# Fifteen taps of one 31-tap convolution chunk as diagonal fp32 products on the matmul engine

## The chip, the cores and the metric

One core of a Trainium2 chip. The metric is the device time of one execution in microseconds. TensorE is called PE, VectorE DVE, ScalarE ACT, GpSimd POOL, SyncE SP.

## The reference, cut to what matters

Two transformer blocks over 512 tokens of width 1024. The second begins with a mixer of two halves: a causal depthwise convolution of 31 taps over 512 channels, followed by a layer norm over the channels and SiLU, and an mLSTM of four heads. Both halves are joined and multiplied by `w_out`; a mixture of 32 experts follows.

```python
u = conv_a * jax.nn.sigmoid(conv_gate)
u = causal_depthwise_conv(u, conv_w, conv_b)      # width 31, one filter per channel
u = jax.nn.silu(layernorm(u, conv_ln_g, conv_ln_b))
...
y = jnp.concatenate([u, hm], axis=-1)             # hm: the four mLSTM heads
return jnp.einsum("bse,ed->bsd", y, w_out)
```

All values are fp32.

## The kernel before

Activations lie transposed: 128 features on the partitions, 512 tokens along a row, one such array being a chunk. The convolution has four chunks (0 to 3), the mLSTM one chunk per head (0 to 3). A product with weights is made from two fp32r parts of either operand, as three matmuls (hi*hi, hi*lo, lo*hi, `terms`, L96). Products of plain fp32 operands take two passes, which the profile shows as two matmuls.

Weight tiles come through a ring of four slots (`ring_load`, L847). `ring_split` (L854) makes the two parts of a tile: ACT copies it to fp32r (L861), POOL subtracts (L864). It is called two tiles ahead, when PE has finished a tile. The mixer has 24 tiles (0 to 23, L1328), made by `feature_tile` (L1256) and `value_tiles` in banks 6, 7 and 2 to 5. `take` (L1275) empties a bank; for the `a` tile of chunk n it writes the gated input `u_pad`, padded by 30 zeros in front, and opens the generator `conv_taps(n)` (L1034): one ACT instruction for tap 0 and the bias, then 30 DVE instructions `dst += w_j * u_pad[j : j + 512]` (L1043), each waiting for the one before.

Eight tiles of the output product follow (24 to 31, `out2_tile`, L1346), as (half i of the output's columns, pair of input chunks). Order: (0,2), (0,3), (1,2), (1,3), (0,0), (0,1), (1,0), (1,1). Pairs 2 and 3 are the heads, pairs 0 and 1 the convolution. Each tile is made in four quarters of 128 tokens, six matmuls each; with pair 2 the residual is added through eight small matmuls with the identity per quarter (L1379). Tile 24's last quarter uses a bank that head 3's sums occupy and waits for `taken[3]`; tile 26's last quarter uses bank 7, where the convolution's layer norm makes its sums, and waits for `stats_read`. Tile 25 needs head 3's split, tile 28 the splits of convolution chunks 0 and 1, tile 29 those of 2 and 3.

The order of instructions in every engine's queue is set while the program is built. `clk` holds an estimated clock for PE, ACT and DVE, `est` adds a cost to one, and background work is written as generators that yield the time at which they want to go on. `tick(spent)` (L1227) is called between groups of matmuls: it adds the time to PE's clock, resumes each background generator that is due, and then emits taps as long as DVE's clock is less than 0.8 beyond PE's. Two open convolution chunks give their taps in turn. `until` (L1251) ticks by 0.3 until a thing it needs has been emitted. An engine executes its queue in order, and waits for others through semaphores.

The generators in this stretch are:
- `weigh(h)` (L1053) for head h: scores (L1063), DVE scaling (L1072), products with the values and with ones (L1078, L1081)
- `finish(h)` (L1130): absolute value on ACT (L1134), gate and maximum on DVE (L1136, L1138, `taken`), the sum over features on PE (L1144), centring on DVE (L1148), squares on ACT (L1151, L1153), their sum on PE (L1159), DVE (L1163), square root on ACT (L1166), reciprocal and multiply on DVE (L1169, L1170), split (L313 on ACT, L315 on DVE)
- `conv_norm()` (L1189), which starts when all four chunks are in `convolved`: mean product (8 passes, the first L460 group in the rows), centring on DVE (L1201), squares on ACT (L1202), squares product, statistics (L1209, `stats_read`), square root, reciprocal, and per chunk multiply (L1217), SiLU (L1219) and split.

When tile 27 is done SP loads the first four expert weights of 2 MB (L1410, in the trace L921), when tile 31 is done three more (L1435); the expert stage follows.

Of the kernel before, what the change touches and what calls it, by code (L numbers as in the profile page):

```python
# [21 lines left out]
T, D = 512, 1024  # L22
# [6 lines left out]
CONV_W, QKC_W = 31, 4  # L29
# [15 lines left out]
ACT, ALU, AX = mybir.ActivationFunctionType, mybir.AluOpType, mybir.AxisListType  # L45
# [83 lines left out]
def build(nc, x_d, cols_d, rows_d, wdense_d, wff_d, wif_d, wr_d, strips_d, experts_d, out_d):  # L129
    sem = nc.alloc_semaphore  # L130
    PE = Queue("pe", nc.tensor, sem("pe_steps"))
    AC = Queue("ac", nc.scalar, sem("act_steps"))
    DV = Queue("dv", nc.vector, sem("dve_steps"))
    PO = Queue("po", nc.gpsimd, sem("pool_steps"))
    SP = Queue("sp", nc.sync, None)
    pe, ac, dv, po, sp = nc.tensor, nc.scalar, nc.vector, nc.gpsimd, nc.sync
# [14 lines left out]
    def sb(name, words, dt=F32, parts=128):  # L151
        return nc.alloc_sbuf_tensor(name, [parts, words], dt)

    def sb2(name, words):

        t = sb(name, words)
        return t, nc.alloc_sbuf_tensor_at(name + "_parts", [128, words], F32R, offset=nc.sbuf_base - words * 4)
# [3 lines left out]
    ident, ones, tri, tri_strict = sb("ident", 128), sb("ones", 128), sb("tri", 128), sb("tri_strict", 128)  # L161
# [8 lines left out]
    att, att_r = sb2("attention_buffers", 8 * T)  # L170
    hi_raw, weights_hi = sb2("weights_hi", 2 * SLOT)
    sumsq, rinv = sb("sum_of_squares", T), sb("token_scale", T)
    banks = [nc.alloc_psum_tensor(f"bank{i}", [128, 512], F32) for i in range(8)]
# [4 lines left out]
    def col(name, k=0):  # L178
        return cols[:, COLS[name] + k:COLS[name] + k + 1]

    def chunk(t, k, n=T, w=T, off=0):

        return t[:, bass.ds(k * w + off, n)]
# [300 lines left out]
    at = {}  # L484
    n = 0
# [349 lines left out]
    clk, due = {"pe": 0.0, "ac": 0.0, "dv": 0.0}, [0.0]  # L835

    def est(q, cost, after=0.0):

        clk[q] = max(clk[q], after or due[0] or clk["pe"]) + cost
        return clk[q]  # L840
# [4 lines left out]
    ring_freed, hi_made, lo_made = {}, {}, {}  # L845
# [33 lines left out]
    m = pe.matmul(banks[0][:, :], ones[:, :], sumsq[:, :], start=True, stop=True)  # L879
# [46 lines left out]
    PU, PQ = T + CONV_W - 1, T + QKC_W - 1  # L926
    at_ = 0

    def part(n):
        nonlocal at_  # L930
        at_ += n
        assert at_ <= BIG - 8 * T
        return big[:, at_ - n:at_]
    u_pad, qk_pad = part(4 * PU), part(4 * PQ)
# [4 lines left out]
    ym = part(8 * T)  # L939
# [15 lines left out]
    dense_read, gated, padded, tapped, convolved, opened = [None] * 8, {}, {}, {}, {}, {}  # L955
    scored, summed_up, taken, var_read, split, split_u, silus = {}, {}, {}, {}, {}, {}, {}
    v2_ready, rows_ready, sig_read, stats_read = [], [], [selectors], {}
    floored = {}
    next_taps, x_ready = [], []
    dense_done, rows_at, taps_at, tick_at = [], [], {}, []  # L960


# [71 lines left out]
    def conv_taps(c):  # L1034

        AC.wait(gated[c])
        last = AC.step(ac.activation(chunk(ym, c), u_pad[:, c * PU:c * PU + T], ACT.Identity,  # L1037
                                     scale=col("conv_w", c * CONV_W), bias=col("conv_b", c)))
        began = est("ac", 0.65)
        for j in range(1, CONV_W):  # L1040
            src, w, dst = u_pad[:, c * PU + j:c * PU + j + T], col("conv_w", c * CONV_W + j), chunk(ym, c)
            DV.wait(last, gated[c] if j == 1 else None)
            last = DV.step(dv.scalar_tensor_tensor(dst, src, w, dst, ALU.mult, ALU.add))  # L1043
            clk["dv"] = max(clk["dv"], began) + 0.85
            yield
        convolved[c] = last


    weights = [W(3), W(4)[:, 0:384], W(5)[:, 0:256], W(4)[:, 384:512]]
# [175 lines left out]
    background, short_taps, long_taps, started, ticks = [], [], [], [0], []  # L1225
# [30 lines left out]
    def feature_tile(i, kind, n):  # L1256

        w = ring_tile(i)
        bank = 6 + i % 2
        PE.wait(dense_read[bank])  # L1260
        for k in range(KD):
            ts = terms(w[:, k * 128:(k + 1) * 128], chunk(nrm_parts, k))
            for j, (x, y_) in enumerate(ts):
                if not ring_freed:
                    PE.wait(ready[k])
                m = pe.matmul(banks[bank][:, :], x, y_, start=k + j == 0, stop=k == KD - 1 and j == 2, skip_group_check=True)  # L1266
            if k == KD - 1:
                if kind in "qk" and n >= 2:
                    until(tapped, n - 2)
                take(kind, n, ring_done(i, m), bank)  # L1270
                ring_split(i + 2)
            if k % 2:
                tick(1.38)

    def take(kind, n, r, bank):  # L1275

        if kind != "a":
            AC.wait(r)
        if kind == "g":
            AC.wait(sig_read[0])  # L1280
            dense_read[bank] = opened["g", n] = AC.step(ac.activation(sumsq[:, :], banks[bank][:, :], ACT.Sigmoid,
                                                                      bias=col("b_conv", 4 + n)))
            est("ac", 2.0)
        elif kind == "a":
            DV.wait(r, opened["g", n])
            gated[n] = sig_read[0] = dense_read[bank] = DV.step(dv.scalar_tensor_tensor(
                u_pad[:, n * PU + CONV_W - 1:(n + 1) * PU], banks[bank][:, :], col("b_conv", n), sumsq[:, :],
                ALU.add, ALU.mult))
            est("dv", 0.8)
            long_taps.append(conv_taps(n))  # L1290
        elif kind == "o":
            dense_read[bank] = opened["o", n] = AC.step(ac.activation(o_gate[n], banks[bank][:, :], ACT.Sigmoid,
                                                                      bias=col("b_o", n)))
            est("ac", 2.0)
        else:
            r_ = kind == "k"
            p0 = (2 * (n % 2) + r_) * PQ
            AC.wait(tapped.get(n - 2))
            dense_read[bank] = padded[kind, n] = AC.step(ac.activation(
                qk_pad[:, p0 + QKC_W - 1:p0 + PQ], banks[bank][:, :], ACT.Identity, bias=col("b_qk", n + 4 * r_)))  # L1300
            est("ac", 0.7)
            if kind == "k":
                next_taps.append(n)
# [100 lines left out]
    for n, (i, pair) in enumerate(tiles):  # L1404
# [16 lines left out]
        if n == 7:  # L1421
            PE.wait(*out_copied[0])
            for k in range(4):
                bank = banks[sums_at[0][k]]
                for t in range(NT):
                    m = pe.transpose(bank[:, t * 128:(t + 1) * 128], x_tok[:, t * D + k * 128:t * D + (k + 1) * 128], ident[:, :])
# [14 lines left out]
    def half_logits(t, i):  # L1441

        return product(halves_of_logits[i][:, t, 0:36],
                       [(h_feat[:, k * T + t * 128:k * T + (t + 1) * 128], wr[:, k * 36:(k + 1) * 36])
                        for k in range(4 * i, 4 * i + 4)])
# [17 lines left out]
    for t in range(NT):  # L1463
        m = half_logits(t, 0)
# [22 lines left out]
    for t in range(NT):  # L1487
        PO.wait(AC.step(ac.activation(h_tok[:, t * D:(t + 1) * D], x_tok[:, t * D:(t + 1) * D], ACT.Identity,
                                      scale=st[:, t:t + 1])))
# [76 lines left out]
    m = pe.matmul(banks[0][:, 0:NT * 32], tri_strict[:, :], both, start=True, stop=False, skip_group_check=True)  # L1566
    for d in range(1, NT):
        m = pe.matmul(banks[0][:, d * 32:NT * 32], ones[:, :], both[:, 0:(NT - d) * 32], start=False, stop=d == NT - 1,
                      skip_group_check=True)
# [351 lines left out]
    for t in range(NT):  # L1921
        for j in range(2):
            c = j * NT + t
# [145 lines left out]
```

How the kernel before makes its waits and increments, by code:

```python
    def run(self, ins):  # L114
        s = self.step(ins)
        self.eng.wait_ge(self.sem, s.value(self.loop))
        return s
# [1 line left out]
    def wait(self, *steps):  # L120
        for s in steps:
            if s is not None:
                self.eng.wait_ge(s.queue.sem, s.value(self.loop))
# [5 lines left out]
def build(nc, x_d, cols_d, rows_d, wdense_d, wff_d, wif_d, wr_d, strips_d, experts_d, out_d):  # L129
# [77 lines left out]
    cleared = PO.run(po.memset(zeros, 0.0))  # L207
    PO.run(po.affine_select(out=ident[:, :], in_=ident[:, :], compare_op=ALU.not_equal, fill=1.0, base=0,
                            pattern=[[-1, 128]], channel_multiplier=1))
    PO.run(po.affine_select(out=tri[:, :], in_=ones[:, :], compare_op=ALU.is_ge, fill=0.0, base=0,
                            pattern=[[1, 128]], channel_multiplier=-1))
    c_ready = PO.run(po.affine_select(out=tri_strict[:, :], in_=ones[:, :], compare_op=ALU.is_gt, fill=0.0,
                                      base=0, pattern=[[1, 128]], channel_multiplier=-1))
    for q in (PE, AC, DV):
        q.wait(c_ready)
        q.eng.wait_ge(s_cols, 16)
    iota_f, tok_id, fold = sb("iota_f", 128), sm(2 * NT), sm(2 * BS)
    PO.run(po.tensor_tensor(fold, ident[:, 0:2 * BS], ident[:, 2 * BS:4 * BS], ALU.add))
    PO.run(po.iota(iota_f[:, :].bitcast(I32), [[1, 128]], base=0, channel_multiplier=0))
# [272 lines left out]
    for k in range(KD):  # L493
        if k % 2 == 0:
            ac.wait_ge(s_x[k // 2], 16)
            dv.wait_ge(s_x[k // 2], 16)
# [32 lines left out]
    dv.wait_ge(s_strip, 16)
    for hh in range(12):
```

## Time and profile before

| | |
|---|---|
| median of three runs | 2053.32 us (2043.6 to 2054.55) |
| profiled execution, its time | 2054.98 us |
| its span, first to last instruction | 2053.7 us |
| mean granted clock of PE | 0.937 |
| PE busy | 1824.7 us (89%) |
| DVE busy | 863.6 us (42%) |
| ACT busy | 432.7 us (21%) |
| POOL busy | 992.7 us (48%) |

The span is 1.3 us shorter than the profiled execution's own time. PE is busy for most of the span, but its load is not even: the mixer and output product lie between about 1190 and 1500 us, the expert stage with its weight transfers behind that. Busy shares say little about one stretch; there the chain that ended last and the timelines of the engines are to be read. Matmuls overlap each other by about 0.17 us in the rows, so the distance of their starts counts, not the sum of their times. The granted clock is 1.00 at 2.4 GHz and 0.50 at 1.2 GHz.

### The profile page before, as it was taken

Reading aid. Unit: us, or ns where it says so; the run is one execution under the profiler, and the core shown is the slowest. Engines: PE = TensorE matmul, PEld = TensorE weight load, DVE = VectorE, ACT = ScalarE, POOL = GpSimd, SP = SyncE. Lnnn points to the kernel's source line nnn. Section 1 sums busy time; section 2 is a strip of 40 time slices with the busy share of each in tenths; the row PEclk is TensorE's granted clock in tenths of the full one; section 3 lists DMA queues with packets and bytes.
Section 4 is the critical chain, followed back from the end, with each engine's and each line's share of the span. In section 5 each row is a group of like instructions: output and inputs, shape, how many; then the busy total and the mean of one; then the engine's idle time right before and its main releaser. Section 6 shows DMA issues by size and latency. Waiting matters only on the chain.

```text
span 2053.7 us, 27415 instructions
## 1 busy us (share of the span) xinstructions
PE 1824.7 (89%) x9686; PEld 1287.1 (63%) x9686; DVE 863.6 (42%) x1256; ACT 432.7 (21%) x794; POOL 992.7 (48%) x536
## 2 busy tenths in 40 slices
PE   5999999989999899999999798996877978969783
PEld 4888888877776578888888666664642423323331
DVE  5444443410254567444444489877341111111113
ACT  3111100100244432111100143551321211111112
POOL 5888887767544278888888523321211111101101
PEclk9999999999999999999999999997868988988897
DMA  3333363423221123333333222210579999999983
GB/s 126 97 97 93 105 262 98 141 79 98 66 62 52 32 85 95 97 93 101 92 109 98 72 60 64 72 52 21 212 287 412 374 408 402 410 415 398 413 358 133
DMA packets 56977, 346.00 MB, mean 168 GB/s; under 512 B 8474, under 2 KB 8858, under 8 KB 44896
## 3 DMA queue, kind: packets, MB, share of 16 engines
q1 hardware_dynamic: 44640, 315.12, 42.1%
q10 hardware_dynamic: 7968, 19.46, 2.6%
q0 software_dynamic: 4320, 10.78, 1.5%
q8 instruction: 29, 0.48, 0.1%
q14 instruction: 20, 0.16, 0.0%
HBM read 475.06 MB, written 19.66 MB: 241 GB/s over the span
## 4 chain that ended last, share of the span: by engine, by line
PE 70%; DMA 13%; DVE 11%; ACT 3%; issue 1%; POOL 1%; SPq 0%; DVEq 0%; ACTq 0%; POOLq 0%
PE bank L460 31%; DMA big<-w_up_in 13%; PE bank L431 12%; PE bank L1760 7%; PE bank L692 4%; PE bank L1266 3%; DVE big L1043 3%; PE bank L1778 2%; PE bank L479 2%; PE bank L1376 2%; PE bank L1786 1%; PE bank L610 1%; DVE state L1028 1%; PE bank L670 1%; PE bank L1678 1%
## 5 line engine op out<-in xcount | busy, mean ns | idle before, releaser
L277 POOL TENSOR_TENSOR weights_hi_parts<-ring,ones 128x1024 fp32r<-128x1024 f32 (+1 forms) x176 | 356.6, 2026 | 304.7 <-PE bank L460 139.1
L279 POOL TENSOR_TENSOR ring_parts<-ring,weights_hi_parts 128x1024 fp32r<-128x1024 f32 (+1 forms) x176 | 473.9, 2693 | 13.8
L460 PE MATMUL bank<-attention_buffers_parts,weights_hi_parts 128*128 128x512 f32 x832 | 329.4, 396 | 27.9 <-POOL ring_parts L279 17.6
L460 PE MATMUL bank<-state_parts,weights_hi_parts 128*128 128x512 f32 x832 | 326.8, 393 | 0.0
L460 PE MATMUL bank<-attention_buffers_parts,ring_parts 128*128 128x512 f32 x832 | 326.7, 393 | 0.0
L1760 PE MATMUL bank<-big,work 128*32 128x512 f32 x1440 | 231.7, 685 | 54.5 <-DMA big<-w_up_in 54.4
L431 PE MATMUL bank<-big_parts,weights_hi_parts 128*128 128x512 f32 x704 | 217.1, 389 | 1.2 <-POOL ring_parts L279 1.2
L460 PEld LDWEIGHTS bank<-attention_buffers_parts,weights_hi_parts 128*128 128x128 f32 x832 | 158.1, 190 | 64.6 <-POOL ring_parts L279 17.6
L864 POOL TENSOR_TENSOR ring_parts<-ring,weights_hi_parts 128x1024 fp32r<-128x1024 f32 x32 | 81.0, 2534 | 234.1 <-ACT weights_hi_parts L861 234.1
L1860 POOL TENSOR_TENSOR small<-small 128x1 f32<-128x1 f32 x51 | 9.7, 190 | 381.3 <-DVE small L1683 381.3
L460 PEld LDWEIGHTS bank<-state_parts,weights_hi_parts 128*128 128x128 f32 x832 | 158.3, 190 | 33.4 <-issue 0.8
L460 PEld LDWEIGHTS bank<-attention_buffers_parts,ring_parts 128*128 128x128 f32 x832 | 158.0, 190 | 33.5
L1719 DVE TENSOR_TENSOR work<-bank,cols 128x256 f32<-128x256 f32 x54 | 22.9, 425 | 306.0 <-PE bank L1678 304.9
L431 PEld LDWEIGHTS bank<-big_parts,weights_hi_parts 128*128 128x128 f32 x704 | 132.0, 188 | 29.2 <-POOL ring_parts L279 2.0
L1760 PEld LDWEIGHTS bank<-big,work 128*32 128x32 f32 x1440 | 63.6, 123 | 135.3 <-issue 129.6
L431 PE MATMUL bank<-big_parts,ring_parts 128*128 128x512 f32 x352 | 136.9, 389 | 0.0
L406 DVE TENSOR_TENSOR work<-bank,token_scale 128x512 f32<-128x512 f32 x44 | 30.4, 692 | 199.9 <-PE bank L460 199.9
L1043 DVE SCALAR_TENSOR_TENSOR big<-big,cols 128x512 f32<-128x512 f32 x120 | 106.5, 929 | 6.4 <-ACT big L1037 5.3
L315 DVE TENSOR_TENSOR big_parts<-work,big_parts 128x512 f32 (+1 forms) x44 | 82.9, 1884 | 42.3 <-ACT big_parts L313 42.3
L1792 ACT ACTIVATE weights_hi<-bank 128x512 f32<-128x512 f32 x54 | 32.3, 598 | 312.1 <-PE bank L1760 312.1
L1760 PE MATMUL bank<-attention_buffers,work 128*32 128x512 f32 x288 | 75.0, 667 | 24.0 <-DMA big<-w_up_in 23.4
L313 ACT ACTIVATE big_parts<-work 128x512 f32 (+1 forms) x44 | 27.9, 633 | 287.3 <-DVE work L408 287.3
(377 smaller groups left out, 2827.1 us busy)
## 6 DMA issues: line engine op xcount, KB each, us to landing
big<-w_up_in SPq DMA_DIRECT2D x54, 2048.0 KB
ring<-wdense_in SPq DMA_DIRECT2D x176, 512.0 KB, 3.6
state<-w_down_in SPq DMA_DIRECT2D x37, 2048.0 KB
big<-w_gate_in SPq DMA_DIRECT2D x36, 2048.0 KB
attention_buffers<-w_gate_in SPq DMA_DIRECT2D x18, 2048.0 KB
ring<-w_down_in SPq DMA_DIRECT2D x18, 2048.0 KB
ring<-wff_in SPq DMA_DIRECT2D x32, 704.0 KB, 4.1
y_rows<-big ACTq DMA_DIRECT2D x1, 8192.0 KB, 28.0
```

The source lines that it names most:

```text
L277: po.tensor_tensor(hi, raw, ones[:, 0:1].to_broadcast([128, words]), ALU.mult).then_inc(PO.sem, 1)
L279: po.tensor_tensor(lo, raw, hi.bitcast(F32), ALU.subtract) \
L315: return DV.step(dv.tensor_tensor(lo, raw, hi.bitcast(F32), ALU.subtract))
L431: m = pe.matmul(bank, x, y_, start=t + k + n == 0, stop=t == 1 and k == h - 1 and n == 2)
L460: m = pe.matmul(out, x, y_, start=j + n == 0, stop=j == len(pairs) - 1 and n == len(ts) - 1)
L479: m = pe.matmul(banks[t][:, :], x, y_, start=k + n == 0, stop=k == KD - 1 and n == len(ts) - 1)
L692: m = pe.matmul(banks[7][:, :], x, y_, start=k + t == 0, stop=k == KD - 1 and t == 2, skip_group_check=True)
L864: lo_made[n] = PO.step(po.tensor_tensor(lo, raw, hi.bitcast(F32), ALU.subtract))
L1043: last = DV.step(dv.scalar_tensor_tensor(dst, src, w, dst, ALU.mult, ALU.add))
L1266: m = pe.matmul(banks[bank][:, :], x, y_, start=k + j == 0, stop=k == KD - 1 and j == 2, skip_group_check=True)
L1376: m = pe.matmul(bank[:, :], x, y_, start=k == 4 and n == 0, stop=k == 3 and n == 2, skip_group_check=True)
L1760: m = pe.matmul(first_products[b][p:p + BS, :], xet[:, (k + odd) * BS:(k + odd + 1) * BS], sets[b][m_][:, (k + odd) * D_EXP:(k + odd + 1) ...
```

## The change

The DVE taps of convolution chunk 3 stop 15 earlier. Once the mixer's last tile is done, ACT makes 15 diagonal matrices of 128x128 in `att`, which held an operand of the mixer: the identity, each row scaled by that channel's weight of taps 16 to 30. PE multiplies each with the shifted input and sums all 15 products in bank 7; plain fp32, so two passes each. One DVE instruction adds the bank to the 16 taps that ACT and DVE made. The generator `pe_taps` emits five diagonals per tick, then one product per tick, and adds 0.88 per product to PE's estimated clock. `convolved[3]` is now set by the addition.

```diff
--- before.py
+++ after.py
@@ -956,7 +956,7 @@
     scored, summed_up, taken, var_read, split, split_u, silus = {}, {}, {}, {}, {}, {}, {}
     v2_ready, rows_ready, sig_read, stats_read = [], [], [selectors], {}
     floored = {}
-    next_taps, x_ready = [], []
+    next_taps, x_ready, own_taps, PE_TAPS = [], [], [], 15
     dense_done, rows_at, taps_at, tick_at = [], [], {}, []
 
 
@@ -1037,13 +1037,46 @@
         last = AC.step(ac.activation(chunk(ym, c), u_pad[:, c * PU:c * PU + T], ACT.Identity,
                                      scale=col("conv_w", c * CONV_W), bias=col("conv_b", c)))
         began = est("ac", 0.65)
-        for j in range(1, CONV_W):
+        for j in range(1, CONV_W - (PE_TAPS if c == 3 else 0)):
             src, w, dst = u_pad[:, c * PU + j:c * PU + j + T], col("conv_w", c * CONV_W + j), chunk(ym, c)
             DV.wait(last, gated[c] if j == 1 else None)
             last = DV.step(dv.scalar_tensor_tensor(dst, src, w, dst, ALU.mult, ALU.add))
             clk["dv"] = max(clk["dv"], began) + 0.85
             yield
-        convolved[c] = last
+        if c < 3:
+            convolved[c] = last
+        else:
+            own_taps.append(last)
+
+    def pe_taps():
+
+        while not dense_done:
+            yield 0
+        AC.wait(gated[3], ring_freed[23])
+        made = []
+        for n in range(PE_TAPS):
+            d = att[:, n * 128:(n + 1) * 128]
+            made.append(AC.step(ac.activation(d, ident[:, :], ACT.Copy, scale=col("conv_w", 3 * CONV_W + CONV_W - PE_TAPS + n))))
+            at = est("ac", 0.33)
+            if n % 5 == 4:
+                yield 0
+        PE.wait(dense_read[7])
+        for n in range(PE_TAPS):
+            j = 3 * PU + CONV_W - PE_TAPS + n
+            PE.wait(made[n])
+            m = pe.matmul(banks[7][:, :], att[:, n * 128:(n + 1) * 128], u_pad[:, j:j + T], start=n == 0, stop=n == PE_TAPS - 1,
+                          skip_group_check=True)
+            clk["pe"] += 0.88
+            if n < PE_TAPS - 1:
+                yield 0
+        m = PE.step(m)
+        at = clk["pe"]
+        while not own_taps:
+            yield 0
+        yield at
+        DV.wait(m, own_taps[0])
+        convolved[3] = DV.step(dv.tensor_tensor(chunk(ym, 3), chunk(ym, 3), banks[7][:, :], ALU.add))
+        est("dv", 0.8)
 
 
     weights = [W(3), W(4)[:, 0:384], W(5)[:, 0:256], W(4)[:, 384:512]]
@@ -1288,6 +1321,8 @@
                 ALU.add, ALU.mult))
             est("dv", 0.8)
             long_taps.append(conv_taps(n))
+            if n == 3:
+                background.append([pe_taps(), 0.0])
         elif kind == "o":
             dense_read[bank] = opened["o", n] = AC.step(ac.activation(o_gate[n], banks[bank][:, :], ACT.Sigmoid,
                                                                       bias=col("b_o", n)))
```

## Rows read from the trace of the kernel before

**Rows 1.** The page, section 4: the chain that ended last, share by engine.

```profile
PE 70%; DMA 13%; DVE 11%; ACT 3%; issue 1%; POOL 1%; SPq 0%; DVEq 0%; ACTq 0%; POOLq 0%
```

**Rows 2.** The chain from 1376 to 1500: start us, us, what.

```profile
1388.87 3.27 DVE work L1169
...
1428.16 0.76 DVE big L1043
...
1429.17 3.69 PE bank L460 x8
...
1444.66 5.49 PE bank L1376 x24
...
1450.25 1.06 ACT weights_hi_parts L861
...
1457.29 19.31 PE bank L1376 x72
```

**Rows 3.** Timeline of PE, 1376 to 1444: start, us, instructions, [idle before <-releaser].

```profile
1379.29 0.67 PE L1063 MATMUL bank<-state 128*128 128x256 f32 x2 [1.96 <-DVE work L1072]
...
1383.25 1.02 PE L1159 MATMUL bank<-state,ones 128*128 128x512 f32 x2
...
1395.78 0.79 PE L1376 MATMUL bank<-weights_hi_parts,big_parts 128*128 128x512 f32 x1 [3.85 <-DVE work L1138]
...
1403.41 1.13 PE L1159 MATMUL bank<-state,ones 128*128 128x512 f32 x2 [1.45 <-ACT state L1151]
1413.95 0.79 PE L1376 MATMUL bank<-weights_hi_parts,big_parts 128*128 128x512 f32 x1 [9.41 <-DVE big_parts L315]
...
1429.17 3.67 PE L460 MATMUL bank<-big,ones 128*128 128x512 f32 x8 [0.45 <-DVE big L1043]
1436.08 5.25 PE L460 MATMUL bank<-big,ones 128*128 128x512 f32 x8 [3.24 <-ACT big L1202]
```

**Rows 4.** Timeline of DVE, 1376 to 1457.

```profile
1378.47 1.34 DVE L1072 SCALAR_TENSOR_TENSOR work<-bank,work 128x512 f32<-128x512 f32 x3
...
1382.24 4.71 DVE L1043 SCALAR_TENSOR_TENSOR big<-big,cols 128x512 f32<-128x512 f32 x7
...
1413.81 15.11 DVE L1043 SCALAR_TENSOR_TENSOR big<-big,cols 128x512 f32<-128x512 f32 x17
...
1451.86 2.42 DVE L315 TENSOR_TENSOR big_parts<-big,big_parts 128x512 fp32r<-128x512 f32 x1 [3.03 <-ACT big_parts L313]
```

**Rows 5.** Groups of DVE's instructions by line, from 1376 to 1490.

```profile
L1043 DVE SCALAR_TENSOR_TENSOR big<-big,cols 128x512 f32<-128x512 f32 x40 | 33.1, 862 | 0.5
```

**Rows 6.** Timelines of ACT, 1373 to 1380, and of GpSimd, 1445 to 1455.

```profile
1374.10 0.51 ACT L1112 ACTIVATE work<-work 128x128 f32<-128x128 f32 x2
1374.49 0.37 ACT L1114 ACTIVATE work<-bank,small 128x128 f32<-128x128 f32 x1
...
1379.42 0.62 ACT L1153 ACTIVATE work<-work 128x512 f32<-128x512 f32 x1
...
1451.38 2.35 POOL L864 TENSOR_TENSOR ring_parts<-ring,weights_hi_parts 128x1024 fp32r<-128x1024 f32 x1 [3.10 <-ACT weights_hi_parts L861]
```

**Rows 7.** Stretches of PE: us, busy (instructions), granted clock, DMA share, GB/s.

```profile
1377.00:1380.00 3.00, 1.04 (x5) 1.00 0.54 150
1380.00:1383.00 3.00, 3.00 (x10) 1.00 0.06 25
1398.00:1401.00 3.00, 3.00 (x11) 0.50 0.00 0
1416.00:1419.00 3.00, 3.00 (x9) 0.54 0.00 0
1437.00:1440.00 3.00, 3.00 (x6) 0.63 0.00 0
```

**Rows 8.** Timeline of the DMA queue of SP, 1440 to 1500.

```profile
1450.82 0.33 SPq L921 DMA_DIRECT2D attention_buffers<-w_gate_in  x1
...
1483.82 0.33 SPq L921 DMA_DIRECT2D big<-w_up_in  x1
```

## The prediction

> **What bounds the kernel now.** The chain that ended last gives 70% of the span to PE and 13% to expert weights [rows 1]. The change lies in one stretch, between the mixer's last weight tile (its products end at 1377.3) and tile 28 of the output product at 1457.29, so I read the chain piece by piece there [rows 2], then each engine. "Tile 24" to "tile 31" are the eight weight tiles of the output product.
>
> The chain [rows 2]: head 2's reciprocal (1388.87), head 3's finish (its split at 1413.9), taps alone on DVE to 1428.93, the mean product of the layer norm (1429.17), the squares product, tile 27 (1444.66), the split of tile 29's weights on ACT (1450.25), then 7.04 us of splits of the first two normalised chunks until tile 28 starts at 1457.29 with 72 matmuls in 19.31.
>
> PE's order [rows 3] shows what hides behind that chain. PE is idle 1.96, 3.85, 1.45, 9.41, 3.24 us, and 7.2 before tile 28. Tile 25 needs head 3's split and starts at 1413.95; tile 25 (24 matmuls) and three quarters of tile 26 (18, and 24 small ones) fill PE to 1428.7, and the mean product follows at 1429.17. So the taps at the tail are covered almost wholly by PE: taking DVE's tail away alone would let the product start 0.45 us earlier. The gain must come from another order on PE.
>
> DVE runs the two last chunks' taps in turns, 0.67 each (7 in 4.71), and the last chunk alone at 0.79 [rows 4]. Of the last 45 taps 40 come after the mixer's tiles [rows 5]; the order is fixed when the program is built, so I followed the planner's own costs, before and after.
>
> **Removed.** 15 taps, all from DVE's tail of 17 (15.11 us [rows 4]), since the chunks alternate: tap 15 of chunk 3 now falls beside the last one of chunk 2. That is 15.11 less two taps of 0.67: 13.8 us of DVE.
>
> **Added, with its place.** (a) ACT: 15 scalings of 128x128, queued behind the step that ends at 1380.04. Nearest rows: 0.51 for two without a pointer operand, 0.37 for one with [rows 6]; start to start 0.2 to 0.37, I take 0.3. The first is there at 1380.4, the last at 1384.5. ACT is otherwise idle until head 2's square root, so they cost only their first latency. The page "ScalarE: Activation LUTs" of the Trainium skill (What ACT_TABLE_LOAD costs) would make it about 0.29 each, an estimate of 4.4 us in all; no row here shows this form.
>
> (b) PE: 15 fp32 products, each like the 1.02 us row of two passes [rows 3], 0.86 from start to start. Bounds: 12.9 us at full clock, 25.7 at half. By the planner one goes out per tick: four ahead of head 3's last score, one behind head 2's squares product, four between the parts of tile 24, one behind it, three ahead of head 3's squares product, two behind.
>
> (c) The first four stand in front of what was critical. Before, head 3's score started at 1379.29. Now: 1380.4 + 3.4 = 1383.8. PE is idle for 3.1 us ahead of them. After 1.96 idle the granted clock stayed at 1.0 (2.4 GHz), after 3.24 it fell to 0.5 (1.2 GHz) [rows 3, 7]; 3.1 is nearest to 3.24. The squares product then took 5.25 against 3.67 for the same eight passes at full clock, so I take 1.6: score at 1385.4, 6.1 late. The Trainium skill ("TensorE: Matmul & The Clock Gate", What's actually happening) says the throttled state is the default and activity releases it; by that rule every burst behind a longer wait starts slow, and the sum would be the one just made. Without it the sum is 1.6 better.
>
> (d) Who waits behind that: DVE's scaling of the score is ahead of ten taps in its queue, so DVE idles from 1379.2 to 1385.9. Then ten taps 6.7, centring 0.6, three taps 2.0, reciprocal 3.3, and 2.0 of multiply and split: head 2 is split at 1401.0 (before 1394.3, 2.2 behind its reciprocal). Head 3's maximum ends at 1403.0; last quarter of tile 24 2.3, one product 0.86, head 3's sum 0.86: 1407.0. This was 1401.97, at half clock. Centring and square 1.3, but PE first does three products (1409.6), then the squares product (1410.5) and two more: 1412.2. The new addition on DVE, queued ahead of head 3's reciprocal, 0.7: 1412.9. Reciprocal and multiply 4.1: 1417.0.
>
> (e) By the planner the mean product (3.45) now stands ahead of tile 25 and starts at 1412.9, 16 us earlier, inside the old 9.41 us gap. The price: its four centrings on DVE (2.5) and squares on ACT come ahead of head 3's split, which ends 1421.4. Tile 25 starts 7.4 us late, after some 5 us of idle PE, so at half clock again. Its first 4.8 us were at half clock before too (2.4 lost [rows 7]); I keep that. 5.5 + 2.4: 1429.3. The squares product follows without a gap: 1432.8. Tile 26 needs 2.3 per quarter (6 matmuls at 0.229 from [rows 2], 24 in 5.49, and 8 small ones 0.9): end 1441.9, before 1444.7. The statistics, root, reciprocal and first SiLU (7 us) lie under tile 26.
>
> (f) What is late next: the first split is queued on ACT behind tile 28's weight split, which waits for tile 26. From there it is the same 7.04 us as before, the 2.42 us subtraction beside GpSimd's own included [rows 4, 6]: tile 28 at 1449.0, 8.3 us earlier. PE idles only about 1.5 us before it, so it starts at full clock: 72 matmuls x 0.229 = 16.5 in place of 19.31, 2.8 gained. But tile 29 now waits: its weight split comes behind the last SiLU, at +11.2, ACT 1.06 and GpSimd 2.35 [rows 2, 6] make it ready at +14.8 behind tile 26's end, where tile 28 ends at +12.6; with latencies 2.4 lost.
>
> **Sum.** -8.3 - 2.8 + 2.4 = -8.7 us at tile 31's end. All behind it moves along: the next expert loads are issued at tile 31's end (1483.82), the first four at tile 27's end (1450.82) [rows 8], and their 8 MB land before tile 31 ends. Profiled execution 2054.98 (span 2053.7, 1.3 around it) gives 2046.3; the median is 1.7 below it, so I predict 2053.3 - 8.7 = 2044.6. One measurement of this kernel can tell 0.5% (10.3 us) from nothing; the three runs shown lie 11 apart, so this forecast sits just inside that bound.
>
> **Rivals.**
> 1. The clock stays up: no fall ahead of the first products (1.6) and tile 25 at full clock (2.4). -12.7, 2040.6. For: the 9.41 gap shrinks to 5, and PE is dense from 1383 to 1412. Against: 3.24 and 3.85 of idle were enough.
> 2. The mean product stays behind tile 26's third quarter. Then tile 25 starts near 1418.2 (no centrings ahead), 14.7 us as before, and the product starts near 1433, four later than 1429.17; with a warmer tile 28 behind, 2.8 less a wait at 29, about 2055. For: the four products ahead of head 3 push just this. Against: the planner's clock passes the mean product one tick before head 3's split, by 0.7 of its units.
> 3. Slower: PE at 1.2 GHz through the whole run of fp32 products. PE is in order, and from 1380.4 to head 3's sum I count 24.2 us of work at full clock. At half clock throughout tile 25 moves another 22.5 us, beyond what the early mean product gives: +13.8, 2067. Each low microsecond costs half: it turns the sign once PE stays low for 17 us more than the 3 I put in, and passes 0.5% at 38. For: rows 7 have a stretch at 0.50 with PE busy all through (1398 to 1401). Against: other fp32 runs at 1380 to 1383 kept 1.00.
>
> The Trainium skill's same page (HAM oscillation) speaks for this change: work put into PE's waits keeps it warm. It gives no time here beyond rival 1.
>
> **Chances.** Forecast 0.50, its own range 2041 to 2048, a quarter of it beyond 10.3 us of gain; rival 1 0.23, all beyond; rival 2 0.20, no change; rival 3 0.07, of it 0.06 slower. Faster 0.36, same 0.58, slower 0.06. The range takes the forecast, rival 1 down to 2038 and the nearer half of rival 2: 2038 to 2053.
>
> **What would show it.** Right: 25 taps after the mixer in place of 40; the first product near 1380.4, score 4.5 to 6 late; mean product near 1412, ahead of tile 25; tile 25 near 1421; tile 28 near 1449, no half clock in it, a short wait at tile 29. Wrong: the mean product behind tile 25's quarters, a clock of 0.50 through the products, or the expert stage not moving with tile 31.

## The result, and the profile of the changed kernel

| | before | changed |
|---|---|---|
| median, measured side by side on one chip | 2053.94 us (2043.6 to 2054.92, 6 runs) | 2042.59 us (2038.07 to 2044.58, 6 runs) |
| profiled execution, its span | 2053.7 us | 2043.3 us |
| mean granted clock of PE | 0.937 | 0.946 |

The medians differ by 11.4 us. The ratio over all these executions is 0.9949, or 10.5 us, with a 95% interval of [0.9929, 0.997]: at the edge of the 0.5% that one measurement of this kernel can tell. The forecast was 2044.6, from 8.7 us less.

The page, section 1, of the changed kernel: busy time of each engine.

```profile
PE 1826.0 (89%) x9716; PEld 1279.5 (63%) x9716; DVE 848.5 (42%) x1242; ACT 436.8 (21%) x809; POOL 991.8 (49%) x536
```

DVE lost 15 us, ACT gained 4; PE has 1.3 more although 30 matmuls came in, because fewer of its other instructions ran at half clock. Busy time does not tell where 11 us went; the stretch behind the mixer does. The mixer's products end at 1378.29 here and ended at 1377.33 before, so from here on "+" is time since that end.

Timeline of PE, 1376 to 1450 (start, us, instructions, [idle before <-releaser]); its counterpart is [rows 3].

```profile
1381.43 5.37 PE L1067 MATMUL bank<-big,attention_buffers 128*128 128x512 f32 x8 [3.14 <-ACT attention_buffers L1059]
...
1414.65 3.67 PE L460 MATMUL bank<-big,ones 128*128 128x512 f32 x8 [0.98 <-DVE big L1078]
...
1449.84 0.47 PE L1411 MATMUL bank<-weights_hi_parts,big_parts 128*128 128x512 f32 x1 [1.76 <-DVE big_parts L315]
```

The first four products stand ahead of head 3's score, and the mean product starts at +36.4 where it started at +51.8. It is now the layer norm that comes before tile 25, as the chain shows.

The chain of the changed kernel, 1405 to 1487 (start, us, what); its counterpart is [rows 2].

```profile
1413.71 0.69 DVE big L1078
1414.40 3.27 DVE work L1202
...
1418.45 0.62 DVE big L1234
1419.09 2.42 ACT big L1235 x4
1421.51 0.53 ACT big_parts L313
1422.06 0.70 DVE big_parts L315
1422.81 7.32 PE bank L1411 x24
1430.13 3.43 PE bank L460 x8
...
1442.74 1.06 ACT weights_hi_parts L861
1443.81 0.53 ACT big_parts L313
1444.36 2.47 DVE big_parts L315
...
1457.11 0.96 ACT weights_hi_parts L861
1458.20 11.17 PE bank L1411 x48
1469.37 1.75 PE bank L1461 x16
1471.12 5.45 PE bank L1411 x24
1476.57 3.49 PE bank L460 x32
```

The addition (L1078), head 3's reciprocal (L1202), then the centrings and the four squares of the norm (L1234, L1235; of the centrings the chain shows one) stand ahead of head 3's split (L315), and tile 25 starts at 1422.81 (+44.5, before +36.6). The squares product (1430.13) follows without a gap. Tile 28 does not stand in this chain, since tile 29's weights are ready later than it ends; it starts at 1449.84 (+71.6, before +80.0).

Timelines of ACT, 1380 to 1386, and DVE, 1386 to 1398; see [rows 4, 6].

```profile
1380.90 4.47 ACT L1059 ACTIVATE attention_buffers<-ident,cols 128x128 f32<-128x128 f32 x15
```
```profile
1387.27 0.42 DVE L1105 SCALAR_TENSOR_TENSOR work<-bank,work 128x256 f32<-128x256 f32 x1 [7.17 <-PE bank L1096]
1387.61 6.71 DVE L1043 SCALAR_TENSOR_TENSOR big<-big,cols 128x512 f32<-128x512 f32 x10
```

DVE stands still for 7.17 us behind the four products, with ten taps queued behind the scaling it waits for.

Stretches of PE in the changed kernel (us, busy (instructions), granted clock, DMA share, GB/s), and in the second fence in the kernel before; [rows 7] are earlier ones.

```profile
1380.00:1383.00 3.00, 1.57 (x3) 0.85 0.32 128
1383.00:1386.00 3.00, 3.00 (x5) 0.58 0.00 0
1398.00:1401.00 3.00, 3.00 (x18) 1.00 0.00 0
1422.00:1425.00 3.00, 2.19 (x6) 0.67 0.02 5
1450.00:1456.00 6.00, 5.56 (x24) 1.00 1.02 414
1477.00:1486.00 9.00, 8.70 (x76) 1.00 0.96 366
```
```profile
1484.00:1487.00 3.00, 3.00 (x29) 1.00 0.74 208
1487.00:1497.50 10.50, 10.50 (x51) 0.50 1.01 428
```

The last rows of both are the same work, the products for the 32 experts' logits right behind tile 31 (64 matmuls with 36 columns and 16 transposes). They take 9.41 us now and took 13.75, for PE fell to half clock 3.2 us into them and does so no more. The whole difference of the two spans, from one landmark to the next:

| us | before | changed | difference |
|---|---|---|---|
| start to the mixer's end | 1377.33 | 1378.29 | +0.96 |
| to tile 31's end | 106.46 | 98.28 | -8.18 |
| the logits' products | 13.75 | 9.41 | -4.34 |
| the rest: routing, experts | 556.16 | 557.32 | +1.16 |
| span | 2053.7 | 2043.3 | -10.4 |

The fuller clock is a part of the 8.18 too: the squares product takes 3.43 in place of 5.25, tile 25 still runs partly at half clock, and tile 28's 24 matmuls take 5.72 in place of 8.42, which the new wait of 2.64 at tile 29 uses up again.

### The profile page after: what moved, and what is told of

It reads as the page before. It is cut to its first block, busy times and chain, and to the rows that moved or that the text cites. A ratio compares the mean times of both kernels' runs of the same rounds, so it can differ in the third digit from the quotient of the medians.

```text
span 2043.3 us, 27479 instructions
## 1 busy us (share of the span) xinstructions
PE 1826.0 (89%) x9716; PEld 1279.5 (63%) x9716; DVE 848.5 (42%) x1242; ACT 436.8 (21%) x809; POOL 991.8 (49%) x536
## 2 busy tenths in 40 slices
DMA packets 56977, 346.00 MB, mean 169 GB/s; under 512 B 8474, under 2 KB 8858, under 8 KB 44896
## 4 chain that ended last, share of the span: by engine, by line
PE 70%; DMA 15%; DVE 10%; ACT 3%; issue 1%; POOL 1%; SPq 0%; DVEq 0%; ACTq 0%; POOLq 0%
PE bank L460 30%; DMA big<-w_up_in 13%; PE bank L431 12%; PE bank L1795 6%; PE bank L692 4%; PE bank L1299 3%; PE bank L479 2%; DVE big L1043 2%; PE bank L1813 2%; PE bank L1411 2%; DMA state<-w_down_in 1%; PE bank L610 1%; PE bank L1821 1%; DVE state L1028 1%; PE bank L670 1%
## 5 line engine op out<-in xcount | busy, mean ns | idle before, releaser
L279 POOL TENSOR_TENSOR ring_parts<-ring,weights_hi_parts 128x1024 fp32r<-128x1024 f32 (+1 forms) x176 | 473.8, 2692 | 13.8
L1795 PEld LDWEIGHTS bank<-big,work 128*32 128x32 f32 x1440 | 59.0, 123 | 141.5 <-issue 140.1
L315 DVE TENSOR_TENSOR big_parts<-work,big_parts 128x512 f32 (+1 forms) x44 | 82.9, 1885 | 42.4 <-ACT big_parts L313 42.4
L1043 DVE SCALAR_TENSOR_TENSOR big<-big,cols 128x512 f32<-128x512 f32 x105 | 91.5, 921 | 4.3 <-ACT big L1037 3.6
```

Source lines behind the costliest of these rows:

```text
L279: po.tensor_tensor(lo, raw, hi.bitcast(F32), ALU.subtract) \
L315: return DV.step(dv.tensor_tensor(lo, raw, hi.bitcast(F32), ALU.subtract))
L1795: m = pe.matmul(first_products[b][p:p + BS, :], xet[:, (k + odd) * BS:(k + odd + 1) * BS], sets[b][m_][:, (k + odd) * D_EXP:(k + odd + 1) ...
```

## The experiments

Theory: the gain is the mean product's earlier place in PE's queue, which a later head 3 and a slow first burst partly give back. Rivals: it is the shorter tail of DVE by itself; or it is the fuller clock (no run holds the clock down with the order kept, so its share is read from the traces alone). Then: does the logits' clock belong to the change?

All twelve runs, each with the kernel before on the same chip; medians of 4 to 11 executions where nothing else is said, the landmarks from the one that was profiled:

| kernel | median us | ratio [95%] | mixer's end | tile 31's end | logits us | rest us |
|---|---|---|---|---|---|---|
| before, once more | 2055.28 (one run) | | 1378.17 | +106.46 | 13.78 | 555.59 |
| changed, once more | 2041.97 | 0.9940 [0.9927, 0.9954] | 1378.27 | +98.29 | 9.42 | 556.62 |
| taps left out | 2042.02 | 0.9947 [0.9933, 0.9960] | 1376.20 | +104.71 | 9.41 | 550.38 |
| mean product held | 2056.84 | 1.0013 [1.0004, 1.0022] | 1374.89 | +109.98 | 13.80 | 554.93 |
| products late | 2041.28 | 0.9938 [0.9924, 0.9952] | 1376.97 | +97.79 | 9.42 | 555.42 |
| split first | 2040.32 | 0.9935 [0.9922, 0.9949] | 1377.53 | +95.41 | 9.41 | 556.65 |
| both of these | 2038.05 | 0.9921 [0.9908, 0.9934] | 1374.83 | +94.46 | 9.42 | 557.39 |
| all three orders | 2033.15 | 0.9895 [0.9880, 0.9909] | 1376.48 | +90.86 | 9.41 | 555.85 |
| fillers | 2035.70 | 0.9918 [0.9904, 0.9932] | 1375.06 | +95.11 | 9.41 | 554.82 |
| tail delayed | 2050.21 | 0.9987 [0.9976, 0.9999] | 1375.24 | +105.75 | 13.19 | 557.02 |
| three orders, fillers | 2030.19 | 0.9886 [0.9871, 0.9901] | 1377.29 | +87.72 | 9.42 | 555.27 |
| three orders, ten taps | 2037.36 | 0.9922 [0.9909, 0.9936] | 1375.03 | +94.08 | 9.42 | 555.37 |

The mixer's end differs by up to 3.5 us between kernels whose code up to there does the same, and the rest by some 2.5. Differences of medians carry that, so small ones are read from the landmarks.

### Taps left out

Taps 16 to 30 of chunk 3 are computed nowhere: no diagonals, no products, no addition.

```diff
-        if c < 3:
-            convolved[c] = last
-        else:
-            own_taps.append(last)
+        convolved[c] = last
...
-            if n == 3:
-                background.append([pe_taps(), 0.0])
```

> Left out: taps 16 to 30 of chunk 3, and with them the 15 diagonals, the 15 products and the addition; DVE has 15 taps less, PE nothing more. The planner puts the mean product where it was before, behind tile 26's third quarter. My theory (the gain comes from the mean product's place on PE, not from DVE's shorter tail): tile 25 starts as before near 1414, the mean product within 1 us of 1429 after the mixer has ended at 1377, tile 28 within 2 us of 1457, the time within 3 us of before (ratio 1.000, 0.998 to 1.001). The rival (13.8 us of DVE were on the path and the products give part of it back) wants 10 us or more off, 2042 or less, since here nothing is given back.

Its timeline of PE, 1412 to 1457:

```profile
1412.82 0.80 PE L1406 MATMUL bank<-weights_hi_parts,big_parts 128*128 128x512 f32 x1 [9.34 <-DVE big_parts L315]
...
1427.51 3.60 PE L460 MATMUL bank<-big,ones 128*128 128x512 f32 x8
...
1455.69 0.77 PE L1406 MATMUL bank<-weights_hi_parts,big_parts 128*128 128x512 f32 x1 [7.16 <-DVE big_parts L315]
```

Tile 25 started at 1412.82 (+36.6), the mean product at 1427.51 (+51.3), tile 28 at 1455.69 (+79.5). Before it was +36.6, +51.8 and +80.0. A DVE tail shorter by 13.8 us, at no price at all, gives 0.5 at the mean product and at tile 28, and 1.8 at tile 31's end (1.3 of it because tile 28 spends less time at half clock), where the changed kernel has 8.2: the shorter tail is not the gain.

The total missed what I expected, 2042.02 in place of 2050 to 2056, and is what the rival asked for. The landmarks say why it does not speak for the rival. In the trace this kernel is 13.0 us below the one before: 1.1 before the mixer's end, 1.8 up to tile 31's end, 4.3 in the logits, which ran at full clock here too, and 5.8 behind them. The logits are taken up under "tail delayed". Behind them the values are others, since taps are missing; but PE has the same 3508 instructions there and the whole kernel moves the same 346.00 MB, so the experts do not have less to do by these counts. Why they took less time is not shown. Such a run can be read up to the logits only.

### Mean product held

The changed kernel with its mean product kept behind tile 26's third quarter, as before.

```diff
-        while len(convolved) < 4 or not dense_done:
+        while len(convolved) < 4 or not dense_done or not at_last_quarter:
             yield 0
...
                 elif i and t == 3:
+                    at_last_quarter.append(True)
                     until(stats_read, 0)
```

> The change with one thing undone: the generator of the layer norm may not begin until tile 26's last quarter asks for it, so the mean product stands on PE where it stood before. Same instructions otherwise, nothing left out. My theory: tile 25 starts 3 us earlier than in the change (no centrings ahead of head 3's split), near 1418 to 1419, the mean product near 1433, four later than before, tile 28 near 1461 less what a warm clock gives; tile 31 ends 0 to 3 us later than before. Time 2053 to 2057, ratio to before 1.000 to 1.002. The rival (shorter DVE tail) wants the gain of the change kept within 3 us: 2040 to 2046.

The chain of this kernel:

```profile
1430.55 3.45 PE bank L460 x8
...
1437.22 5.20 PE bank L460 x8
...
1458.35 19.33 PE bank L1412 x72
```

The mean product at +55.5 in place of +51.8, and behind it everything as in [rows 2, 3]: the squares product at half clock, 72 matmuls in 19.33. Tile 31 ends 11.7 us later than in the changed kernel, and the logits are at half clock again (4.4 more). With the same instructions the median is 14.2 us above the changed kernel's (a ratio to the kernel before of 1.0013 in place of 0.9949): the place of the mean product, with the norm's steps that follow it, is what the gain hangs on.

### Before and changed, once more

No edit in either.

> The kernel before once more, for a second trace of it. Asked: is the granted clock in the router's first products behind tile 31 (L460, 36 columns) again 0.50 from 1488 on, as in the first trace, or 1.00 as in the trace of the change? If it is 1.00 here, the 4.3 us that this stage gave beyond my sum in the change belong to the run and not to the change, and the end lies 3 to 4 us below the first trace's.

> The changed kernel once more, unaltered. If the logits stage's clock belongs to the place in time at which the stage comes and not to chance of one execution: tile 31 ends about 98 us after the mixer stage's end, the logits products take 9.4 us at a granted clock of 1.00, and the median stands about 2042. If it is chance, the stage takes 13.8 us in some executions of this kernel, and this profile may show it.

Both repeat their landmarks within 0.1 us behind the mixer's end (table above), logits included. So the two clocks there are not the chance of one trace each. That every execution is like the traced ones is not shown: one of the first six of the kernel before took 2043.6 us, and one of 15 on the last chip 2043.45, at a mean granted clock of 0.944 where the others had 0.934 to 0.941 (2049.89 to 2055.88 us). No trace of such an execution exists.

### Products late

The fifteen products wait until head 3's score has been issued.

```diff
+        while ("weights", 3) not in opened:
+            yield 0
         PE.wait(dense_read[7])
```

> The change with the products put behind head 3's last score and its value products; diagonals, count and addition as in the change. The planner then puts five products ahead of head 3's first sum, three ahead of its second, six ahead of tile 25, and the mean product behind tile 25. My theory: the first products no longer hold DVE's scaling and the ten taps behind it (7 us in the change), head 2 is split as early as before, tile 25 starts near 1411 after a mixer's end at 1377.3, tile 26 ends near 1433.5, tile 28 starts 7 us behind that, near 1441: about 8 us below the change, 2034 to 2036. The rival (the 12.9 us of products cost the same wherever they stand, since PE is full) wants the time of the change within 2 us.

A miss: 0.5 us at tile 31's end, and a median 1.3 below the changed kernel's. Head 3 is early (score at 1378.95, +2.0, tile 25 at +37.3), but now the mean product comes behind tile 25, at +46.2, and the squares product behind tile 26's second quarter. The first SiLU then falls behind a weight split in ACT's queue.

Its chain:

```profile
1439.39 1.07 ACT weights_hi_parts L861
...
1441.77 0.73 ACT big L1254
...
1445.39 1.06 ACT weights_hi_parts L861
1446.45 0.53 ACT big_parts L313
...
1447.00 2.43 DVE big_parts L315
...
1449.57 10.50 PE bank L1413 x39
```

So the early head and the early mean product compete, and the delay of head 3 that I had counted as a price of the change is also what puts the mean product ahead of tile 25. Tile 26 ends at +61.4, where I had expected +56. The rival's number, the time of the change within 2 us, came true, and this run does not refute it: where the products stand matters little by itself.

### Split first, and both

The layer norm's centring and squares wait until head 3's split has been issued, so the split no longer stands behind them:

```diff
         squares = []
+        mean_out.append(True)
+        while 3 not in split:
+            yield 0
         DV.wait(s)
```

> The change, but the four centrings and squares of the layer norm are emitted behind head 3's split instead of ahead of it; the mean product keeps its place ahead of tile 25. My theory: tile 25 starts 3.1 us earlier (2.5 of centrings on DVE, 0.6 of ACT), all behind it moves by 2.5 to 3.5, about 2039.5. If the split is not what tile 25 waits for, nothing moves.

2040.32: as expected. Tile 25 starts at 1419.13 (+41.6) behind 1.57 us of waiting in place of 4.48, tile 28 at +67.1, and tile 29 then falls to half clock behind a wait of 2.67.

With this, the products late, and tile 25 held until the mean product has been issued:

```diff
+            while n_tile == 25 and not mean_out:
+                tick(0.3)
             for k in (2 * pair, 2 * pair + 1):
```

> Products behind head 3's scores, mean product ahead of tile 25, head 3's split ahead of the centrings. By the PE sum (tile 26 ends when its, tile 25's and both norm products are done, from about 1411.7) tile 26 ends at 1433 as in the kernel with late products alone: 2033 to 2036, and the place of the mean product no longer matters, because the norm's chain lies under tile 26 in both.

2038.05, above the 2033 to 2036: tile 26 ends at +60.5, where I had expected about +56. Tile 28 is as early as in "split first" (+66.7), tiles 27 and 28 run without a gap, and tile 29 comes behind a wait of 2.24. At tile 31's end the late products are worth 0.9 us beside "split first". That the mean product's time would no longer matter was wrong: the chain runs from it (1412.93) through tile 25 and the squares product to the norm, and the mean product itself took 5.31 us in place of 3.45, largely at half clock.

### All three orders

As "both", and the last SiLU waits in ACT's queue behind tile 29's weight split:

```diff
         for k in range(4):
+            while k == 3 and 29 not in hi_made:
+                yield 0
             s = DV.step(dv.scalar_tensor_tensor(chunk(ym, k), chunk(ym, k), col("ln_g", k), spread
```

> As the kernel with late products and split first, and the weight split of tile 29 queued on ACT ahead of the last SiLU. In the change tile 29 waited 2.64 us for that split. My theory: 1.5 to 2.5 us below the same kernel without it. If tile 29 then waits for the last chunk's split instead, less than 1 us.

The chains of "both" (first) and of "all three orders", from the split that tile 29 waits for:

```profile
1446.76 2.45 DVE big_parts L315
...
1449.35 12.74 PE bank L1418 x48
```
```profile
1447.56 1.29 DVE big_parts L315
1448.85 0.14 issue
1448.99 11.15 PE bank L1420 x48
```

3.6 us earlier at tile 31's end, more than expected: 2.0 of the wait (2.24 to 0.20) and 1.6 that I had not counted, since PE stays at full clock for want of a wait (11.15 for the 48 matmuls, 12.74 before). 2033.15 is below both kernels.

### Fillers

Products of no use into bank 6, 14 pairs ahead of the first tap products and 20 pairs ahead of tile 25.

```diff
+    def filler(count):
+        PE.wait(dense_read[6])
+        for _ in range(count):
+            pe.matmul(banks[6][:, 0:128], ones[:, :], ident[:, :], start=True, stop=True, skip_group_check=True)
+    filler(14)
...
+            if n_tile == 25 and t == 0:
+                until(split, 3)
+                filler(20)
```

> The change with 14 matmuls of ones with the identity ahead of the first product and 20 ahead of tile 25, into a bank that nobody reads, 0.22 us each at full clock: PE works while it would wait, nothing else moves. My theory of the clock: the granted clock stays 1.00 in the first products (4 in 3.4 us in place of 5.2) and in tile 25 (5.5 in place of 7.3), so tile 28 starts 3 to 3.5 us earlier: 2039 to 2040. If the fall was not from the wait, the clock falls all the same and the fillers cost 0 to 1 us.

Its timeline of PE, 1374 to 1415:

```profile
1374.91 3.29 PE L1377 MATMUL bank<-ident,ones 128*128 128x128 f32 x28
1378.21 3.67 PE L1067 MATMUL bank<-big,attention_buffers 128*128 128x512 f32 x8
...
1413.26 4.63 PE L1377 MATMUL bank<-ident,ones 128*128 128x128 f32 x40
```

The first four products take 3.67 in place of 5.37, tile 28 starts at +68.4 in place of +71.6, and tile 31 ends 3.2 earlier, as the landmarks were expected. The two falls cost the changed kernel 3.2 us; I had put them at 4.0. The median is lower than expected by some 4; the mixer's end, ahead of any filler, was 3.2 earlier in this profile.

### Tail delayed

The changed kernel with 33 filler pairs ahead of tile 26 (7.37 us), so that tile 31 ends about as late as before.

```diff
             bank = banks[sums_at[i][t]]
+            if n_tile == 26 and t == 0:
+                filler(33)
```

> The changed kernel with 33 extra product pairs of no use (about 7.3 us of TensorE by the rows of the earlier filler run) ahead of tile 26, which push tile 31's end back to about where it was before the change, 105.5 us after the mixer stage's end. Nothing of the logits stage is altered. Theory A (the logits stage fell to half clock before the change, and not after it, because of when it comes after the earlier work): the logits products take 13.8 us again and the total is about 11.4 us above the changed kernel, near 2054. Theory B (the full clock in the logits stage has another cause, for one that the products keep TensorE busier): 9.4 us as in the changed kernel, and the total is 7.3 us above it, near 2050.

Its stretches of PE in the logits, and the one of "taps left out":

```profile
1481.50:1484.50 3.00, 3.00 (x29) 1.00 0.82 251
1485.00:1494.00 9.00, 9.00 (x44) 0.50 1.00 428
```
```profile
1481.00:1490.00 9.00, 8.71 (x78) 1.00 0.91 350
```

Theory A in the trace: with tile 31's end at +105.75 the logits fall to half clock 3.9 us in and take 13.19, and from the mixer's end to the end of the span it is 675.96 against 664.33 in the changed kernel's second trace, taken on the same chip: 11.6 us more. The median rose by 8.2 only, between the two theories; the mixer's end lay 3.0 us earlier in this kernel's profile, which makes up most of the difference. "Taps left out", whose tile 31 ended at +104.71, ran the same logits at full clock. So nothing in the change itself speeds the logits up: the time at which they come decides. That earlier than about +105 is always good is not shown. The fall came at +109.6 to +109.7 in six traces whose tile 31 ended anywhere from +97.8 to +106.5, so it does not follow tile 31's end. A rival stands untested: not how late the logits come decides, but where they lie relative to the clock's earlier changes. Delays of other lengths would tell the two apart; none was run.

### Three orders with fillers, and with ten taps

```diff
         yield 0
+        filler(12)
         PE.wait(*convolved.values(), dense_read[7])
...
                     until(taken, 3)
+                    filler(10)
```

> The fastest version so far (products behind head 3's score, mean product behind head 3's weight split, tile 29's split ahead of the last SiLU; 2033.15 median, mean product 38.1 us after the mixer stage's end, tile 31's end at +90.9) with filler products in the two waits after which the granted clock fell. If the two half-clock stretches cost what the filler run showed for them (3.1 to 3.5 us in all), tile 31 ends at about +87.5, the granted clock is 1.00 from the mixer stage to the logits, and the median is near 2030. Rival: in this version VectorE's chain to the mean product sets the time, so the fillers only fill waits and gain nothing: 2033.

One stretch of PE holds all of it, from the mixer to the logits:

```profile
1377.00:1474.00 97.00, 94.53 (x466) 1.00 0.38 146
```

Full clock throughout, +87.72 and 2030.19: both as expected. This is the fastest kernel of the study, 1.1% below the one before. Its own rival, that fillers only fill waits, falls.

```diff
-    next_taps, x_ready, own_taps, PE_TAPS = [], [], [], 15
+    next_taps, x_ready, own_taps, PE_TAPS = [], [], [], 10
```

> The fastest version so far with 10 taps on TensorE and 15 more left with VectorE (five taps go back to VectorE, three of them ahead of head 3's reciprocal and two behind its split). If VectorE's count of taps sets the mean product's time, as the prediction priced it at 0.67 to 0.9 us for each, then the mean product comes 3 to 4 us later (about +41.5 after the mixer stage's end) and the median is near 2036. Rival: the last stage is bound by TensorE's own work, and fewer products (5 x 0.43 to 0.86 us) give back as much: 2033 or below.

The mean product came at 1416.18, +41.2 in place of +38.1, and tile 31 ended 3.2 later: DVE's five taps set it (0.6 us each), and the five products less bring nothing back. The median, 2037.36 in place of 2033.15, fits the 2036 expected. The split between the engines does matter once the orders are right.

## Why the prediction was right, step by step

The time was right within 2.0 us, the difference (11.4 for 8.7) with one term missing. That it came so close is luck in part: of the 4.3 us that were missing, the experts gave 1.2 back and the mixer's end 1.0 in the profiled execution. The mechanism up to tile 31's end was right. Less the 0.96 us by which the mixer ended later:

| step | predicted | measured, less 0.96 |
|---|---|---|
| (a) a scaling; first product | 0.3; 1380.4 | 4.47 / 15 = 0.30; 1380.5 |
| (b) where the 15 products stand | 4, 1, 4, 1, 3, 2 | 4, 1, 4, 1, 3, 2 |
| (c) head 3's score | 1385.4 | 1385.7 |
| (d) end of the products | 1412.2 | 1412.7 |
| (e) mean product, ahead of tile 25 | 1412.9 | 1413.7 |
| (e) tile 25; tile 26's end | 1421.4; 1441.9 | 1421.9; 1441.7 |
| (f) tile 28; wait at tile 29 | 1449.0; 2.4 | 1448.9; 2.64 |
| tile 31's end | -8.7 | -8.2 |

**(a), (b).** DVE has 25 taps behind the mixer's end, as counted. The estimate from the Trainium skill ("ScalarE: Activation LUTs", What ACT_TABLE_LOAD costs), 0.29 us for a scaling, agrees with 0.30 here.

**(c).** PE waited 3.14 us (I had 3.1) and fell to half clock: four products in 5.2 from start to start, 1.7 above full clock, for my 1.6. The Trainium skill ("TensorE: Matmul & The Clock Gate", What's actually happening) says that the throttled state is the default and that activity releases it; the trace agrees at this place and at tile 25 (behind 4.48 us). At tile 29 PE stayed at full clock behind 2.64 us.

**(e).** The half clock at tile 25 cost 1.8 (7.32 for 5.5) and not 2.4.

**(f).** Tile 28 ran at full clock, and the new wait at tile 29, queued behind the last SiLU, came as it was worked out. "All three orders" took it away and shows that it was worth 2 us.

**The step that failed is the last one, "all behind it moves along".** The logits did not: 4.3 us came from their clock. I had looked at the clock in each stretch up to tile 28 and not once behind it, though the kernel before shows 0.50 from 1487.0 on. The experts gave 1.2 back; 0.9 of it lies between the logits' end and the routing's first small product (11.56 us earlier, then 10.69), where DVE's small steps set the time. With both terms the sum would have been -8.7 - 4.3 + 1.2 = -11.8, beside the 11.4 measured.

**Rival 1** (clock stays up, 12.7 less) did not come true by itself. "Fillers" forced it: 3.2 us at tile 31's end where I had 4.0. **Rival 2** (mean product behind tile 26's third quarter, about 2055) is what "mean product held" made: 2056.84, and its argument, four products that push head 3, was the wrong way round: a later head 3 lets the mean product pass. **Rival 3** (half clock throughout the products) is excluded by the stretch at 1398 to 1401 at 1.00. Behind the first four, all products ran at full clock (1.00 from 1386 to 1422).

**The chances.** The result lies at the bound: a ratio of 0.9949, where I had given 0.36 to more than 0.5% of gain. A quarter of the forecast's 0.50 beyond the bound was low, since the missing term pointed to that side.

## What to carry to other kernels

When an engine's tail is covered by another one's queue, shortening it gives little (0.5 us at the next product for 13.8 here); ask which instruction the change lets pass which other. Move work that frees time, then put right each order that it disturbs: three orders, put right by four waits in the planner, made 2033 of 2042. And follow the clock to the end of the program's dense part: here a stage lost a third of its time by coming 8 us earlier, with nothing changed in it.

## What the runs showed of the hardware that I had not expected

- The length of a wait alone does not decide whether PE falls to half clock. It stayed up behind 2.64 us (tile 29, changed kernel; 2.63 in "fillers") and fell behind 2.24 ("both") and 2.67 ("split first") at the same tile.
- A dense run of narrow products can fall too. With 36 columns each and no idle time, the logits fell in each of the four traces of this study in which tile 31 ended at +105.7 or later and in none of the ten where it ended at +104.7 or earlier; 9.4 or 13.2 to 13.8 us. That lateness as such is the cause is not shown ("tail delayed").
- In six executions (before twice, changed twice, products late, tail delayed) that fall came 109.6 to 109.7 us after the mixer's end, whether PE was then in the logits or already done with them. In the others it came elsewhere, between 99.5 and 116.7. What it is tied to, no run here settles.
- Fifteen 128x128 copies on ACT with a scale per partition take 0.30 us each back to back.
- With the taps left out, what follows the logits took 550.4 us in place of 554.8 to 557.4 in the other traces, with as many PE instructions and as many bytes moved. Other values are what differs; how they shorten it stays open.
